# Attention of a hybrid trunk kernel: one head at a time, or two heads on the two halves of TensorE's array

## What is computed

```python
D_MODEL = 1024; SEQ = 128; DEC_SEQ = 512; PAST_LEN = 128
BLOCK = 128; WINDOW = 128
ATTN_HEADS = 8; KV_HEADS = 2; HEAD_DIM = 64

def window_attention(q, k, v, k_ctx, v_ctx, sink):
    ...
    s_loc = jnp.einsum('bnqkgd,bnskd->bnkgqs', qb, kb).astype(jnp.float32) * scale
    s_loc = jnp.where(valid[None, :, None, None], s_loc, -jnp.inf)
    s_ctx = jnp.einsum('bnqkgd,bckd->bnkgqc', qb, k_ctx).astype(jnp.float32) * scale
    ...
    p = jax.nn.softmax(jnp.concatenate([s_loc, s_ctx, sink_l], axis=-1), axis=-1)
    ...
    o = (jnp.einsum('bnkgqs,bnskd->bnqkgd', p_loc, vb)
         + jnp.einsum('bnkgqc,bckd->bnqkgd', p_ctx, v_ctx))
    return o.reshape(b, t, D_ATTN)

def modulation(cond, w, b):
    m = jax.nn.silu(cond) @ w + b
    return jnp.split(m[:, None, :], 6, axis=-1)
```

## Time and profile before

| | |
|---|---|
| median of 3 executions | 4232.13 us |
| the profiled execution | 4240.17 us, of which its span is 4238.4 us |
| attention, from the first constant load to the first load of the scan | 271.8 to 442.1 us, 170.3 us |
| busy share of the span | PE 73%, DVE 65%, ACT 38%, POOL 35% |
| mean granted TensorE clock | 0.874 of 2.4 GHz |
| memory traffic | 1507.71 MB, mean 356 GB/s |

### The profile page before, as it was taken

The page is one execution under the profiler, slowest core; times in us unless marked ns, Lnnn a source line. Parts: engine busy times, 40 slices in busy tenths (PEclk is TensorE's granted clock), DMA queues, the critical chain, the costliest instruction groups (busy, mean ns, idle before and its releaser), DMA issues.

```text
span 4238.4 us, 67991 instructions
## 1 busy us (share of the span) xinstructions
PE 3094.2 (73%) x25020; PEld 1480.9 (35%) x25020; DVE 2741.8 (65%) x6901; ACT 1603.3 (38%) x4953; POOL 1482.1 (35%) x1298
## 2 busy tenths in 40 slices
PE   7989888877875555578975777897685675666555
PEld 5644777433331111134521433452251241132111
DVE  2645444776666676676975656787756786756764
ACT  2524322343333243244642334563333363322332
POOL 0000000244344444443543444454434444444443
PEclk9989999999997777789987988998798798888787
DMA  4147101799999999999999999999999999999998
GB/s 163 43 168 272 34 5 52 307 419 420 420 416 414 418 413 421 420 412 416 409 407 360 413 419 420 418 418 412 397 419 421 420 419 414 416 419 416 417 421 342
DMA packets 229786, 1507.71 MB, mean 356 GB/s; under 512 B 32238, under 2 KB 33353, under 8 KB 58961
## 3 DMA queue, kind: packets, MB, share of 16 engines
q0 software_dynamic: 184768, 1342.45, 76.8%
q1 hardware_dynamic: 44248, 160.80, 10.0%
q10 hardware_dynamic: 442, 0.12, 0.0%
HBM read 1500.17 MB, written 3.10 MB: 355 GB/s over the span
## 4 chain that ended last, share of the span: by engine, by line
DMA 42%; PE 19%; DVE 10%; ACT 5%; issue 4%; POOL 2%; another core or an unknown queue 0%; SPq 0%; ACTq 0%; POOLq 0%; PEldq 0%; DVEq 0%
DMA t_ring<-in_peer_uv,t_eidx 41%; PE t_ps L2400 10%; DVE t_ring L1728 6%; PE t_ps L2278 2%; POOL t_ring L1590 2%; ACT t_dg L1919 1%; PE t_ps L2297 1%; ACT t_wgt L1913 1%; PE t_ps L2356 1%; PE t_ps L2326 1%; DMA t_wq<-in_cv_w_pw 1%; ACT t_wgt L1908 1%; PE t_ps L2401 1%; DVE t_pair L1791 0%; PE t_ps L2142 0%
## 5 line engine op out<-in xcount | busy, mean ns | idle before, releaser
L1590 POOL DMA_INDIRECT t_ring<-in_peer_uv,t_eidx x1280 | 1474.6, 1152 | 2725.7 <-PE t_ps L2403 1791.9
L2400 PE MATMUL t_ps<-t_ring,t_dg 64*64 64x512 f32 x2560 | 1552.9, 738 | 995.0 <-ACT t_dg L1919 951.6
L1728 DVE SCALAR_TENSOR_TENSOR t_ring<-t_ring,t_hring 128x1024 f32<-128x1024 f32 x1024 | 1255.1, 1226 | 773.8 <-DMA t_ring<-in_peer_uv,t_eidx 719.6
L2403 PE MATMUL t_ps<-t_ring,t_dg 64*64 64x512 f32 x2560 | 1569.6, 745 | 0.0
L2402 PE MATMUL t_ps<-t_ring,t_dg 64*64 64x512 f32 x2560 | 1569.3, 745 | 0.0
L2401 PE MATMUL t_ps<-t_ring,t_dg 64*64 64x512 f32 x2560 | 1569.2, 745 | 0.0
L2400 PEld LDWEIGHTS t_ps<-t_ring,t_dg 64*64 64x64 f32 x2560 | 343.5, 155 | 1983.0 <-issue 1954.5
L1908 ACT ACTIVATE t_wgt<-t_dots 128x2 f32<-128x2 f32 x640 | 130.3, 204 | 1918.3 <-DVE t_ring L1728 1882.4
L1919 ACT ACTIVATE t_dg<-t_eye,t_wgt 128x64 f32<-128x64 f32 x1280 | 375.9, 340 | 1.3 <-ACT t_wgt L1913 1.1
L2403 PEld LDWEIGHTS t_ps<-t_ring,t_dg 64*64 64x64 f32 x2560 | 344.4, 155 | 0.0
L2401 PEld LDWEIGHTS t_ps<-t_ring,t_dg 64*64 64x64 f32 x2560 | 344.2, 155 | 0.0
(11 more groups left out here) (380 smaller groups left out, 4445.5 us busy)
## 6 DMA issues: line engine op xcount, KB each, us to landing
at_ring<-in_mod_w SPq DMA_DIRECT2D x40, 1024.0 KB, 5.1
t_wq<-in_peer_w_q SPq DMA_DIRECT2D x62, 512.0 KB
t_ring<-in_peer_uv,t_eidx POOLq DMA_INDIRECT x1280
t_wg<-in_cv_w_pw SPq DMA_DIRECT2D x32, 512.0 KB
t_wq<-in_cv_w_pw SPq DMA_DIRECT2D x24, 512.0 KB
fr_wring<-in_ab_w_in SPq DMA_DIRECT2D x21, 512.0 KB, 3.5
ev_mod_ring<-in_mod_w SPq DMA_DIRECT2D x8, 1024.0 KB, 18.4
t_wg<-in_peer_w_q SPq DMA_DIRECT2D x16, 512.0 KB
```

The lines of the kernel that those rows point to most:

```text
L1590: pool.indirect_dma_start(ring[:, place[n], :], None, table, bass.IndirectOffsetOnAxis(ap=eidx[:, s % 2, r:r + 1], axis=0)).then_inc(row_i ...
L1728: V.scalar_tensor_tensor(ring[:, place[n], 0:D], ring[:, place[n], 0:D], 1.0, h_of(j), ALU.mult, ALU.mult, accum_out=dots[:, j % 2, r:r + ...
L2400: nc.tensor.matmul(straight[low], diagonal[low], row[low, 0:512], **ends)
L2403: nc.tensor.matmul(crossed[low], diagonal[high], row[high, 512:D], **ends).then_inc(S["used"], 1)
```

## The change

PE, DVE and ACT now take two items, g = 0 and g = 1 of the same `t` and `c`, as a pair. There are 20 pairs.

- `scores(m)` issues the two cached-key matmuls and then the two local-key matmuls, rows 0 to 63 and 64 to 127 in turn, each into its own bank of `ps_s`. It waits until both items of the pair before have been masked.
- `turn` is called twice, then `weigh(m - 1)` alternates between the groups for every tile, and two modulation steps follow.
- `s` and `st` have four places, so masking waits for the transposes of item n - 4. The space comes from `rot`, which now lies in places 2 and 3 of `s`, and from `sink`, which moves to a spare piece of `u`.
- DVE masks both items of a pair, normalises both, and does a modulation group after pairs 3, 7, 11, 15 and 19. ACT does both exponentials and then both copies of the pair before.
- The constants are loaded in another order and counted by three semaphores: `keys_in` (cached keys, permutation) for PE's first work, `rope_in` for DVE's rotation, `rest_in` (mask, sink, cached values) for the first masking and the first weighing.

```diff
+self.spare = u[:, 14, 0:HEADS]
...
-sink, rot = sb("sink", [P, HEADS]), sb("rot", [P, 2, T_LAT])
-s, pT = sb("s", [P, 2, 4 * P]), sb("pT", [P, 2, 4 * P])
-st = sb("st", [P, 2, 6])
+sink = scan_parts.spare
+s, pT = sb("s", [P, 4, 4 * P]), sb("pT", [P, 2, 4 * P])
+rot = s[:, 2:4, :]
+st = sb("st", [P, 4, 6])
...
-    sp.dma_start(perm[:], K.const["ropeperm"]).then_inc(const_in, 16)
-    sp.dma_start(rope[:].rearrange("p a t -> p (a t)"), K.const["rope"]).then_inc(const_in, 16)
-    sp.dma_start(kctx[:], io["cache_k"][0, 0].rearrange("t g e -> t (g e)")).then_inc(const_in, 16)
-    sp.dma_start(vctx[:], io["cache_v"][0, 0].rearrange("t g e -> t (g e)")).then_inc(const_in, 16)
-    sp.dma_start(mask[:], K.const["amask"]).then_inc(const_in, 16)
-    sp.dma_start(sink[:], io["ab_sink"][0].partition_broadcast(P)).then_inc(const_in, 16)
+    sp.dma_start(kctx[:], io["cache_k"][0, 0].rearrange("t g e -> t (g e)")).then_inc(keys_in, 16)
+    sp.dma_start(perm[:], K.const["ropeperm"]).then_inc(keys_in, 16)
+    sp.dma_start(rope[:].rearrange("p a t -> p (a t)"), K.const["rope"]).then_inc(rope_in, 16)
+    sp.dma_start(mask[:], K.const["amask"]).then_inc(rest_in, 16)
+    sp.dma_start(sink[:], io["ab_sink"][0].partition_broadcast(P)).then_inc(rest_in, 16)
+    sp.dma_start(vctx[:], io["cache_v"][0, 0].rearrange("t g e -> t (g e)")).then_inc(rest_in, 16)
...
-    pe.wait_ge(const_in, 96)
+    pe.wait_ge(keys_in, 32)
...
-    def scores(n):
-        t, c, g = items[n]
-        if n >= 2:
-            pe.wait_ge(masked, n - 1)
-        rows = slice(g * HD, (g + 1) * HD)
-        q = qT[rows, c, t * P:(t + 1) * P]
-        tiles = blocks[t][1]
-        at = 0
+    def scores(m):
+        t, c, _ = items[2 * m]
+        if m:
+            pe.wait_ge(masked, 2 * m)
+        tiles, at = blocks[t][1], 0
+        groups = [(g, slice(g * HD, (g + 1) * HD)) for g in range(KV)]
...
-            nc.tensor.matmul(ps_s[:, n % 2, 0:P], q, kcT[rows, :], start=True, stop=True)
+            for g, rows in groups:
+                nc.tensor.matmul(ps_s[:, g, 0:P], qT[rows, c, t * P:(t + 1) * P], kcT[rows, :], start=True, stop=True)
...
-        nc.tensor.matmul(ps_s[:, n % 2, at:at + width], q, kT[rows, tiles[0] * P:tiles[0] * P + width],
-                         start=True, stop=True).then_inc(s_done, 1)
+        for g, rows in groups:
+            nc.tensor.matmul(ps_s[:, g, at:at + width], qT[rows, c, t * P:(t + 1) * P], kT[rows, tiles[0] * P:tiles[0] * P + width],
+                             start=True, stop=True).then_inc(s_done, 1)
...
-            last = nc.tensor.transpose(ps_t[:, n % 2, b * P:(b + 1) * P], s[:, n % 2, b * P:(b + 1) * P], ident[:])
+            last = nc.tensor.transpose(ps_t[:, n % 2, b * P:(b + 1) * P], s[:, n % 4, b * P:(b + 1) * P], ident[:])
...
-    def weigh(n):
-        t, c, g = items[n]
-        pe.wait_ge(p_copied, n + 1)
-        if c == 0 and g == 0 and t >= 2:
+    def weigh(m):
+        t, c, _ = items[2 * m]
+        pe.wait_ge(p_copied, 2 * m + 2)
+        if m == 0:
+            pe.wait_ge(rest_in, 48)
+        if c == 0 and t >= 2:
...
-            v = vctx[:, g * HD:(g + 1) * HD] if kt is None else kvtok[:, kt, g * HD:(g + 1) * HD]
-            last = nc.tensor.matmul(ps_o[g * HD:(g + 1) * HD, t % 2, c * P:(c + 1) * P], v, pT[:, n % 2, b * P:(b + 1) * P],
-                                    start=(b == 0), stop=(b == len(tiles) - 1))
-        last.then_inc(o_done, 1)
+            for g in range(KV):
+                rows = slice(g * HD, (g + 1) * HD)
+                v = vctx[:, rows] if kt is None else kvtok[:, kt, rows]
+                last = nc.tensor.matmul(ps_o[rows, t % 2, c * P:(c + 1) * P], v, pT[:, g, b * P:(b + 1) * P],
+                                        start=(b == 0), stop=(b == len(tiles) - 1))
+                if b == len(tiles) - 1:
+                    last.then_inc(o_done, 1)
...
-    N = len(items)
+    pairs = len(items) // 2
...
-    for n in range(N + 2):
-        if n + 1 < N:
-            scores(n + 1)
-        if 1 <= n <= N:
-            turn(n - 1)
-        if n >= 2:
-            weigh(n - 2)
-        if n < MOD_ITEMS:
-            modulation((MOD_EARLY + n) // KD, (MOD_EARLY + n) % KD)
+    for m in range(pairs + 1):
+        if m + 1 < pairs:
+            scores(m + 1)
+        if m < pairs:
+            for g in range(KV):
+                turn(2 * m + g)
+        if m:
+            weigh(m - 1)
+        for step in range(MOD_EARLY + 2 * m, min(MOD_EARLY + 2 * m + 2, MOD_STEPS)):
+            modulation(step // KD, step % KD)
...
-    dve.wait_ge(const_in, 96)
+    dve.wait_ge(rope_in, 16)
...
-        p = n % 2
+        p = n % 4
...
-        if n >= 2:
-            dve.wait_ge(p_turned, n - 1)
-        nc.vector.tensor_tensor_reduce(out=s[:, p, 0:width], in0=ps_s[:, p, 0:width], in1=mask[:, first * P:first * P + width], scale=1.0,
+        if n == 0:
+            dve.wait_ge(rest_in, 48)
+        if n >= 4:
+            dve.wait_ge(p_turned, n - 3)
+        nc.vector.tensor_tensor_reduce(out=s[:, p, 0:width], in0=ps_s[:, g, 0:width], in1=mask[:, first * P:first * P + width], scale=1.0,
...
-        p = n % 2
+        p = n % 4
...
-    for n in range(len(items) + 1):
-        if n < len(items):
-            mask_scores(n)
-        if n:
-            normalise(n - 1)
-        for g in range(MOD_LATER):
-            if n == (g + 1) * KD - MOD_EARLY + 1:
-                modulation(g)
+    for m in range(len(items) // 2):
+        for g in range(KV):
+            mask_scores(2 * m + g)
+        for g in range(KV):
+            normalise(2 * m + g)
+        if m % 4 == 3:
+            modulation(m // 4)
...
-    for n in range(N):
+    def exponents(n):
...
-        p, width = n % 2, len(blocks[t][1]) * P
+        p, width = n % 4, len(blocks[t][1]) * P
...
-        if n >= 1:
-            copy_p(n - 1)
-        if n >= 10 and n % 8 == 2:
-            copy_o(n // 8 - 1)
-    copy_p(N - 1)
+    for m in range(N // 2 + 1):
+        for g in range(KV):
+            if m < N // 2:
+                exponents(2 * m + g)
+        for g in range(KV):
+            if m:
+                copy_p(2 * m - 2 + g)
+        if m >= 5 and m % 4 == 1:
+            copy_o(m // 4 - 1)
```

More of the change, by code:

```diff
@@ L713, in phase_attention @@
         ps_o = mem.enter_context(nc.psum_tensor("at_ps_o", [P, 2, 512], F32))
-        const_in, kv_turned, kv_copied, kv_out = (K.sem("at_" + n) for n in ("const_in", "kv_turned", "kv_copied", "kv_out"))
+        keys_in, rope_in, rest_in, kv_turned, kv_copied, kv_out = (K.sem("at_" + n) for n in ("keys_in", "rope_in", "rest_in", "kv_turned", "kv_copied", "kv_out"))
         rot_done, rot_step, roped = (K.sem("at_" + n) for n in ("rot_done", "rot_step", "roped"))
```

## The result

| | before | the change |
|---|---|---|
| median | 4233.70 us, 4 runs (4227.99 to 4239.31) | 4195.69 us, 4 runs (4193.00 to 4198.02) |
| ratio, 95% interval | | 0.9911 [0.9893, 0.9928] |
| profiled execution | 4240.17 us | 4194.77 us |
| its span, granted clock | 4238.4 us, 0.874 | 4192.9 us, 0.876 |
| attention: first load of a constant to the scan's first matmul | 271.80 to 442.17: 170.4 us | 271.65 to 398.05: 126.4 us |

The change is faster by 0.9%, 38 us, against the 4193 us and the range of 4182 to 4219 of the forecast. The profiled executions differ by 45.4 us, of which 44.0 lie in the attention; nothing behind it gives any of it back.

The account below looks back on a forecast made before the run. Memory bounds the attention up to 319.6 us, PE alone from 382 to 427. Start, pairs and tail put the scan at 402.3 us, 39.8 less; with 39 taken, 4201 profiled, median 4193 us, range 4182 to 4219.

Parts of the forecast that it names:

- The overlap: Two groups' scores and weighings run side by side: 1.06 and 1.02 us per 4-tile pair, against 1.96 and 1.88 without overlap.
- The clock: PE's clock stays low through the 1-tile pairs (5.7 us each) and rises in the first 3-tile pair (8.3 us).
- The sum: The attention's stages added up, from its start to the scan's first load: 402.3 us against 442.1, 39.8 us less.
- clock full from the start: Rival, chance 0.10: PE waits less for constants, 1-tile pairs go at the loads' 4.92 us; 47 us less, 4185.
- Memory: In the 3-tile pairs the DMA needs until 329 us for the loads, so it is ahead of PE's 337.5.
- the signs that would have shown the forecast wrong: PE waiting for `ring` loads in the 4-tile stretch, a granted clock under 0.9 there, or a longer scan and expert phase.
- The start: Ahead of the pairs, the last early modulation step ends at about 290.5 us, where it ended at 293.1 before.
- The reorder's price: At the attention's start, the new order of constants with three semaphores is worth 3 us, not 8.
- DVE's groups: Modulation groups between pairs delay PE's scores: 3.0 us in the 3-tile pairs, 2.8 and 1.4 in the 4-tile pairs.
- The tail: After the last modulation step: last scores, DVE's masking and normalising, last group, store and its landing; 12.5 us with hand-overs.
- clock stays low: Rival, chance 0.05: packed work leaves PE with gaps, all pairs run at the lower clock; 12 us more than now, 4244.

Follow-up runs that it names:

- the half loads: The change, with each modulation step loading half of its 1024 KB and computing with that half twice; 4183.01 us, 0.9890 of before.
- both halves apart: The change, with the two groups' scores parted by a transposition and their weighings by a modulation step; 4214.95 us, 0.9966 of before.

## Why the prediction held, and where its terms were off

Ends of the stages by PE, as forecast and as the profile of the change has them:

| stage | forecast end | length | measured end | length |
|---|---|---|---|---|
| start of the loop | 290.5 | | 292.8 | |
| four 1-tile pairs | 313.3 | 22.8 | 314.1 | 21.3 |
| four 3-tile pairs | 337.5 | 24.2 | 334.3 | 20.2 |
| eight 4-tile pairs | 381.2 | 43.7 | 375.9 | 41.6 |
| two 3-tile pairs | 389.8 | 8.6 | 385.2 | 9.3 |
| tail | 402.3 | 12.5 | 398.0 | 12.8 |

- **The overlap** was right, both halves of it. Scores of 1.07 us and weighing of 1.03 for two 4-tile items stand where the lower bounds 1.06 and 1.02 were taken, and the pair of 4.95 us where 4.94 was worked out. The Trainium skill, "TensorE: Matmul & The Clock Gate", Part 3, states that a weight load overlaps running matmuls only where the row groups differ; it also says that one can be pulled ahead when it goes to the background weight buffer. The prediction worked out a weighing of 1.88 us from the first of these alone; the runs do not agree with it: 1.03 together, 2.04 apart. Full overlap of two row halves with 128 output columns each, for which no row stood before, takes 1.07 together and 2.14 apart.
- **The clock** was mis-sized. The forecast let it rise in the first 3-tile pair; it rose at about 301 us. The sum had priced the 1-tile pairs at 5.7 us and one 3-tile pair at 8.3. In the change they go at the pace of the loads, about 5 us: 1.5 less in all for the 1-tile pairs; for the 3-tile pairs 3.3 less in the first, some 2 more in the other three, and 3.0 less since DVE's group hides behind the loads. The rival "clock full from the start" had this pace, but the first 1-tile pair still ran at 0.50. The 0.58 of the earlier trace rows, from which the sum took a low clock for all small items, was the mean of a stretch that begins at 1.00 and holds PE's wait of 3.79 us for a load; the prediction does not name this wait.
- **Memory** was taken to be ahead of PE from the 3-tile pairs on ("by 329"). With PE faster there, memory is full until 375.9 us (share 1.01), and the loads set the pace of both 3-tile and 1-tile pairs; the half loads show it, with 11.0 us less. Of the signs that would have shown the forecast wrong none is there: no wait for `ring` and no clock under 1.00 in the 4-tile stretch. In the 4-tile pairs the two limits lie together, 4.95 us by PE and 4.92 by loads.
- **The start** was 2.3 us late: the fourth early step's load came at 290.98, and the step ran at the lower clock. The reorder's price, 3 us, measured 2.1 in the change and 3.7 in the kernel before.
- **DVE's groups** were priced too high: 2.8 and 1.4 us in the 4-tile pairs, 3.0 ahead of them, and waits of some 3 us for the masking, four times. Behind the groups there are two such waits, 0.27 and 0.94 us. Around the long group of the 4-tile pairs, DVE and then PE:

```profile
349.53 2.83 DVE L884 TENSOR_TENSOR at_mod<-at_mps,at_mod 2x512 f32<-2x512 f32 x4
...
353.84 0.75 DVE L862 CUSTOM_DVE_ANT_0 at_s<-at_ps_s,at_mask,ev_u 128x512 f32<-128x512 f32 x1
...
357.35 1.12 PE L789 MATMUL at_ps_t<-ident,at_s 128*128 128x128 f32 x8 [0.64 <-ACT at_pT L914]
```

  The group takes 4.3 us and the masking of two items 1.8 until PE's scores go on at 355.57. The sum put the normalising of both items between them as well, 7.7 us in all, but `scores` waits for the masking only. The pair takes 5.98 us, and the next, whose transposes wait 0.64 us for ACT's copy, 5.68: 1.8 us over 4.95 for this group. The group ahead makes the first 4-tile pair 5.36 us long, 0.4 more, and the short one costs 0.3 in the stretch behind, at 377.09. Together 2.1 us less than the 4.2 of the sum.
- **The tail** was right within 0.4 us. The landing of the store, some 2 us there and read from no row, is 2.6: its issue ends at 393.71 + 1.72 = 395.43 us, and the scan's first load stands at 398.00.
- **The rival "clock stays low"** was said to turn into a loss above two thirds of 14 pairs. Its own numbers, 39.8 us of gain against 52 us of cost, give three quarters. No run reached that.

The sum of 402.3 us for the scan's first load was met with 398.0. The span before it is 44.1 us shorter where 39.8 were worked out, and the medians differ by 38.0 where 39 were taken. Per term the errors are + 2.3 for the start, - 1.5 and - 4.0 for the early pairs, - 2.1 for DVE, + 0.7 and + 0.3 for the end: - 4.3. By cause they are larger and cancel in part: about - 4.8 for the clock's earlier rise, - 4.8 for DVE's groups, + 2.1 for the pace of the loads in the 3-tile pairs, + 2.3 for the start and + 1.0 for the end. The mechanism carried the forecast: the overlaps, the stages and the pace of the 4-tile pairs by PE; the 1-tile and the 3-tile pairs went at the pace of the loads instead. That the medians agree with it within 3 us is in part luck: the saving in the attention was 4.3 us more than the sum, and the profiled executions lay on different sides of their medians. The clock was the one part for which the rows gave no rule.

## What to carry to other kernels

Where PE alone sets the pace and its matmuls use half of the rows or half of the columns, put two independent ones on different halves next to each other, record by record: here the second of each two then cost nothing, 2.1 us of the 7.3 of a 4-tile pair. Before adding it up, compute the distance of the loads, since half of the stages here ended on memory as soon as PE got faster. And look at the granted clock in the stretch behind a wait: here 28 busy us at half speed followed a wait of 3.8 us for a load, and of the 11 us lost in that stretch the wait was the smaller part. That the wait caused the low clock is not shown.

## What the runs showed that was not expected

- Passes on different halves overlap without strict alternation, if few of them stand between: in the weighing two records per group overlap fully, six in part (1.07 us where 0.81 is full), eight in part (1.52 us where 1.03 is full and 2.04 none), and in the scores four per group fully (1.07 us for both groups).
- The lower clock can last through 28 us of PE at 28.00 of 28.00 busy (0.50 from 300 to 328 us before), while in the change, with memory fuller (1.02 against 0.93) and PE less busy (9.54 of 11.50 us, in the row below), it rose at about 301 us:

```profile
288.50:300.00 11.50, 9.54 (x42) 1.92 (x42) 4.03 (x24) 2.81 (x14) 0.00 (x0) 0.50 1.02 393
...
302.00:340.00 38.00, 31.46 (x280) 12.38 (x274) 28.52 (x101) 17.77 (x64) 0.00 (x0) 1.00 1.01 420
```

- The prices of the parts do not add up: 10.8 us for the scores' overlap, 9.0 for the weighing's, 24.4 for both. Where the loads set the pace, as in the 3-tile pairs, a loss of either half is mostly hidden.
- With both halves apart the kernel still has 19.6 of the 44.0 us of the attention.
